# Routing of four expert layers: the gather by halves of the model columns, row products behind the first expert product, other filler counts, three and four down pieces outside the ring

## The chip, the cores and the metric

One core of one Trainium2 chip runs the whole program. The metric is the device time in microseconds of one execution; lower is better. Times of a few executions are given with their median. The profile is of one further execution, and all times inside it are counted from the start of its span.

The engines have the profile's names: PE is TensorE (matrix products), PEld its weight loads, DVE is VectorE, ACT is ScalarE, POOL is GpSimd, SP is SyncE, which here only issues transfers (DMA).

## The reference

Two blocks of two layers each work on 256 tokens of width 1024, in float32. Each layer is a mixer (a gated MLP, attention in several forms) followed by a mixture of experts. The four expert layers are called 0 to 3 here. Layers 0 and 1 (first block) have 32 experts, layers 2 and 3 (second block) have 16. What an expert layer computes, cut to what matters:

```python
def hierarchical_moe(h, ...):                  # h: rms-normed x, 256 x 1024
    g_prob = softmax(t @ w_group + b_group)     # 4 groups
    g_idx = argmax(g_prob); g_w = g_prob[g_idx]
    e_sel = (t @ w_expert + b_expert)[group g_idx]
    top_w, top_i = top_k(softmax(e_sel), 2)     # two experts of the group
    weights = g_w * top_w / sum(top_w)
    # combine: 256 x n_experts, two entries in a row
    gate, up = t @ w_gate[e], t @ w_up[e]       # 1024 -> 256 each
    y = sum_e (silu(gate) * up * combine[:, e]) @ w_down[e]   # 256 -> 1024
x = x + y                                       # second block: x + g_f * y
```

In the second block the normed rows are also scaled and shifted by vectors made from `c` (`w_ada`), and the layer's output is multiplied by a row `g_f`.

## The kernel before, in words

**Weights come as a stream.** All large weights are cut into chunks that SP loads, in one fixed order, into a ring of 24,576 floats in each partition (`Stream`, `ring`). A chunk waits until the chunks that lay in its place have been used: engines count the semaphore `chunk_used` up when they are done with some, and SP waits for a count ahead of each issue. In an expert layer a piece is 1 MiB, so that twelve pieces fill the ring. An expert has three: two with its gate and up weights (rows 0 to 511 and 512 to 1023 of the model columns) and one with its down weights. For the first two experts the down pieces lie outside the ring, in the tile `first_down` (`FIRST_DOWN = 2`, "aside").

**Routing, once in a layer (function `moe`).** PE transposes x (L1502), multiplies it by the router weights (L1514, and ends with `r_ready`), and then issues products of zeros into an unused bank (`keep_busy`, L359). DVE meanwhile picks group and experts (`picks_ready`). PE makes counts from the picks (L1526, L1527), issues twelve more fillers, and DVE makes from the counts the slot of each token for its experts: a one-hot matrix `gather` for each half `t` of the tokens. Then PE gathers the tokens into slots, `xn_split` times `gather` (L1538): for each half t of the tokens the eight blocks k of 128 model columns, two products each (the normed rows are kept as a high and a low part), into four banks. ACT takes banks 0 and 2 of a half (L1720), DVE banks 1 and 3 (`take_gathered`, L1869 or L1872), into `xsT`. PE then turns ranks and weights of the slots into rows (`rows_by_half`, L1546), which ACT copies (L1724, L1726). POOL copies the slots of the first two experts, a pair, out of `xsT` at places known only at run time (L1489): one window of 32 slots for each expert and half of the tokens, all eight k at once. Then the expert products begin.

**Experts, in pairs i.** `gate_up(i, 0)` and `gate_up(i, 1)` are the products over the first and the second four k (L1595); `turn` and `down(i)` (L1604, L1618) follow, and `combine` (L1633) adds rows back to tokens. Each engine branches once in a layer on whether no expert has over 32 slots; the path with windows is the one that the trace shows, the other computes every expert for every token.

**Order.** All instructions of an engine run in the order in which the program has them, held only by semaphores. On ACT the count up of `chunk_used` for the pieces of `gate_up(0, 0)` stands behind everything that ACT has before it. SP's order is: stream up to the layer, first_down, rest of the stream.

## Time and profile before

| | |
|---|---|
| median of 3 runs | 1597.15 us (1593.39 to 1597.97) |
| the profiled execution | 1590.39 us |
| its span | 1588.6 us |
| busy: PE, DVE, ACT, POOL | 1455.9, 758.0, 494.1, 100.9 us |
| moved by DMA | 467.19 MB, mean 294 GB/s |
| mean granted PE clock | 0.977 of full |

The span runs from the first to the last instruction; 1.8 us of the execution lie around it. The page's slices show the transfers at 420 GB/s in most of the expert layers and far below in the mixers, while PE is busy nearly throughout. "Busy" PE time has its waits for data between products left out only where they are long enough to show. The profiled execution is 6.8 us below the median of the runs.

### The profile page before, as it was taken

Reading aid. Unit: us, or ns where it says so; the run is one execution under the profiler, and the core shown is the slowest. Engines: PE = TensorE matmul, PEld = TensorE weight load, DVE = VectorE, ACT = ScalarE, POOL = GpSimd, SP = SyncE. Lnnn points to the kernel's source line nnn. Section 1 sums busy time; section 2 is a strip of 40 time slices with the busy share of each in tenths; the row PEclk is TensorE's granted clock in tenths of the full one; section 3 lists DMA queues with packets and bytes.
Section 4 is the critical chain, followed back from the end, with each engine's and each line's share of the span. In section 5 each row is a group of like instructions: output and inputs, shape, how many; then the busy total and the mean of one; then the engine's idle time right before and its main releaser. Section 6 shows DMA issues by size and latency. Waiting matters only on the chain. (4 is left out here: it accounts for less than half of the span.)

```text
span 1588.6 us, 23901 instructions
## 1 busy us (share of the span) xinstructions
PE 1455.9 (92%) x9314; PEld 808.2 (51%) x9314; DVE 758.0 (48%) x1618; ACT 494.1 (31%) x982; POOL 100.9 (6%) x242
## 2 busy tenths in 40 slices
PE   8999999888899898998888998999999979999997
PEld 4586533222375554322227876787663337756432
DVE  1656432222444635222236655775574346677433
ACT  3222211111215402111126655665412126551211
POOL 0000011010000001111101000100001101000110
PEclk9999999999999999999999998999989999998999
DMA  9985589999963186999997461435079996417996
GB/s 369 369 355 214 236 331 420 421 419 421 404 264 120 50 334 283 420 420 421 421 424 314 178 235 41 158 133 192 24 322 378 420 425 246 151 50 296 387 420 276
DMA packets 62391, 467.19 MB, mean 294 GB/s; under 512 B 7696, under 2 KB 15808, under 8 KB 17472
## 3 DMA queue, kind: packets, MB, share of 16 engines
q1 hardware_dynamic: 62272, 465.59, 72.5%
q8 instruction: 76, 1.25, 0.3%
q14 instruction: 43, 0.35, 0.1%
HBM read 462.81 MB, written 2.76 MB: 293 GB/s over the span
## 5 line engine op out<-in xcount | busy, mean ns | idle before, releaser
L1595 PE MATMUL PS<-ring,catT 128*32 128x512 f32 x3072 | 349.0, 596 | 29.5 <-issue 22.6
L793 PE MATMUL PS<-w_split,h_split 128*128 128x512 f32 x1152 | 271.0, 394 | 6.0 <-DVE w_split L878 6.0
L793 PEld LDWEIGHTS PS<-w_split,h_split 128*128 128x128 f32 x1152 | 214.2, 189 | 56.5 <-DVE w_split L878 8.5
L1595 PEld LDWEIGHTS PS<-ring,catT 128*32 128x32 f32 x3072 | 99.8, 110 | 247.2 <-issue 247.0
L1618 PE MATMUL PS<-ring,hidden_cols 128*32 128x512 f32 x1408 | 159.7, 593 | 29.6 <-issue 24.4
L878 DVE TENSOR_TENSOR w_split<-ring,w_split 128x512 fp32r<-128x512 f32 x192 | 132.7, 706 | 67.4 <-ACT w_split L826 67.2
L826 ACT CAST w_split<-ring 128x512 fp32r<-128x512 f32 x192 | 118.0, 619 | 105.1 <-PE PS L793 104.5
L1765 ACT ACTIVATE hidden_rows<-PS 128x256 f32<-128x256 f32 x48 | 18.5, 384 | 387.6 <-PE PS L1595 387.6
L1618 PEld LDWEIGHTS PS<-ring,hidden_cols 128*32 128x32 f32 x1408 | 47.8, 110 | 134.9 <-issue 134.8
L484 PE MATMUL PS<-ring,catT 128*128 128x512 f32 x224 | 100.8, 610 | 1.0 <-PEq L989 1.0
L413 DVE SCALAR_TENSOR_TENSOR ada_part<-ring,silu_c,ada_part 128x768 f32<-128x768 f32 x98 | 99.9, 1019 | 3.5
L1973 DVE SCALAR_TENSOR_TENSOR xn_split<-PS,slot_w,xn_split 128x512 fp32r<-128x512 f32 x64 | 48.1, 751 | 107.1 <-ACT xn_split L1753 107.0
L1489 POOL COPY catT<-xsT 128x256 f32 x192 | 69.5, 405 | 449.7 <-PE PS L1595 414.4
L1941 DVE TENSOR_TENSOR hidden_rows<-PS,hidden_rows 128x256 f32<-128x256 f32 x48 | 20.3, 422 | 134.4 <-ACT hidden_rows L1765 134.4
L1945 DVE COPY hidden_cols<-PS 128x256 f32<-128x256 f32 x48 | 20.4, 425 | 122.3 <-PE PS L1604 122.3
L1753 ACT ACTIVATE xn_split<-PS,slot_w 128x512 fp32r<-128x512 f32 x64 | 44.0, 688 | 103.3 <-PE PS L1618 103.3
L484 PEld LDWEIGHTS PS<-ring,catT 128*128 128x128 f32 x224 | 43.3, 195 | 54.1 <-issue 54.1
L1966 DVE SCALAR_TENSOR_TENSOR gated_rows<-PS,slot_w,grow 128x512 f32<-128x512 f32 x32 | 24.0, 751 | 83.0 <-PE PS L1618 83.0
L1702 ACT ACTIVATE xn_split<-x 128x1024 fp32r<-128x1024 f32 x8 | 8.5, 1059 | 165.3 <-PEq L454 115.0
L1633 PE MATMUL PS<-xn_split,back 64*128 64x512 f32 x384 | 57.4, 417 | 2.3 <-DVE xn_split L1976 2.1
L1458 POOL MEMSET xsT<- 128x512 f32 x4 | 2.1, 527 | 660.5 <-POOLq L454 524.6
L1633 PEld LDWEIGHTS PS<-xn_split,back 64*128 64x128 f32 x384 | 32.3, 184 | 18.3 <-issue 10.1
(420 smaller groups left out, 1754.1 us busy)
## 6 DMA issues: line engine op xcount, KB each, us to landing
ring<-in_moe SPq DMA_DIRECT2D x280, 1024.0 KB, 16.5
ring<-in_w_ada SPq DMA_DIRECT2D x16, 3072.0 KB, 11.5
ring<-in_a_w_in SPq DMA_DIRECT2D x23, 2048.0 KB, 12.4
ring<-in_b_w_in SPq DMA_DIRECT2D x8, 2048.0 KB, 22.1
first_down<-in_moe SPq DMA_DIRECT2D x8, 1024.0 KB, 17.6
ring<-in_a_w_out SPq DMA_DIRECT2D x2, 3072.0 KB, 10.8
ring<-in_b_w_out SPq DMA_DIRECT2D x2, 3072.0 KB, 9.9
ring<-in_w_mem_kv SPq DMA_DIRECT2D x2, 2048.0 KB, 11.4
```

Of the source, the lines that this page charges most:

```text
L413: dlink(nc.vector.scalar_tensor_tensor(part, w[:, k, :], silu_c[:, k:k + 1], part, ALU.mult, ALU.add))
L484: last = nc.tensor.matmul(PS[:, i % 8, 0:n], srcT[:, j, t * P:(t + 1) * P], w[:, j, o:o + n], start=j == 0, stop=j == k - 1)
L793: last = nc.tensor.matmul(PS[:, 2 * (i % 2) + t, :], hs[:, hp, k, t * P:(t + 1) * P], wk[:, (KT * i + k) % splits, wp, :], start=k == 0 an ...
L826: nc.scalar.copy(wk[:, (KT * i + k) % splits, 0, :], w[:, k, :]).then_inc(w_high.sem, 1)
L878: nc.vector.tensor_tensor(wk[:, (KT * i + k) % splits, 1, :], w[:, k, :], wk[:, (KT * i + k) % splits, 0, :].bitcast(F32), ALU.subtract).t ...
L1489: nc.gpsimd.tensor_copy(xf[:, i % 2, :, q * HALF:(q + 1) * HALF], padded(q // 2)[:, :, bass.ds(at, HALF)]).then_inc(win_ready.sem, 1)
L1595: last = nc.tensor.matmul(PS[lanes, 4 + i % 2, :].rearrange("p (g f) -> p g f", g=2), xf[:, i % 2, k, lanes], gate_up_weights(2 * i + q % ...
L1618: last = nc.tensor.matmul(PS[lanes, 6 + c, :], hs[:, i % 2, f2, lanes], down_weights(2 * i + q % 2)[:, f2, c * BANK:(c + 1) * BANK], start ...
L1633: last = nc.tensor.matmul(PS[:, 2 * t + c, :], back[lanes, i % 2, :], yk(i, h, c)[lanes], start=i == 0 and h == 0, stop=i == NP - 1 and h ...
L1753: nc.scalar.activation(yk(i, 0, c), PS[:, 6 + c, :], ACT.Copy, scale=slot_w[:, i % 2, :]).then_inc(y_high.sem, 1)
L1966: nc.vector.scalar_tensor_tensor(gated[:, c, :], PS[:, 6 + c, :], slot_w[:, i % 2, :], grow[:, c * BANK:(c + 1) * BANK], ALU.mult, ALU.mul ...
L1973: nc.vector.scalar_tensor_tensor(yk(i, 1, c), PS[:, 6 + c, :], slot_w[:, i % 2, :], high, ALU.mult, ALU.subtract).then_inc(y_low.sem, 1)
```

## The change

All in `moe` and what it calls:

- **Gather by halves of the columns.** PE makes for k 0 to 3 both halves of the tokens first, then for k 4 to 7. ACT and DVE take the banks in that order. POOL copies the first pair's windows in two sets of four, with four k each (`first_windows`), and `gate_up(0, 0)` waits for the first set only, `gate_up(0, 1)` for the second. The banks of the second half of the tokens are 4, 5, 6, 7 where they were 6, 7, 4, 5.
- **Row products and weight chain later.** `rows_by_half` for ranks and weights (now `ranks_and_weights`) stands between `gate_up(0, 0)` and `gate_up(0, 1)`; DVE makes ranks and weights after it has taken all banks; ACT copies the rows behind its table load, ahead of the first count up of `chunk_used`.
- **Fillers.** In layers 2 and 3 three instead of ten stand between L1519 and the counts.
- **Down pieces aside.** Three in layer 0, four in layer 1, two in layers 2 and 3. The third (expert 2) goes into `hT`, once the router has read it (`r_ready`); the fourth into `mem_kv`, the tile of the memory's keys and values, which are no longer read after the mixer of layer 1. The path for crowded experts makes its `hT` anew, in `h_again`.

```diff
-FIRST_DOWN = 2
+ASIDE = (3, 4, 2, 2)
-            XB = ((0, 1, 2, 3), (6, 7, 4, 5))
+            XB = ((0, 1, 2, 3), (4, 5, 6, 7))
...
-                aside = FIRST_DOWN
-                first_down = sbuf(st, "first_down", [P, aside, PIECE])
+                aside = ASIDE[m]
+                first_down = sbuf(st, "first_down", [P, 2, PIECE])
+                aside_at = [first_down[:, 0, :], first_down[:, 1, :], hT[:].rearrange("p k t -> p (k t)"), mem_kv[:]][0:aside]
...
-                    for e in range(aside):
-                        nc.sync.dma_start(first_down[:, e, :], A[f"moe{m}"][e][:, 2 * PIECE:3 * PIECE]).then_inc(down_loaded.sem, 16)
+                    for e in sorted(range(aside), key=lambda e: e == 2):
+                        if e == 2:
+                            sp.wait_ge(*r_ready.at(1))
+                        nc.sync.dma_start(aside_at[e], A[f"moe{m}"][e][:, 2 * PIECE:3 * PIECE]).then_inc(down_loaded.sem, 16)
                     stream.issue(nc, sp, first + 3 * E - aside)
...
+                    def first_windows(starts):
+                        pool.wait_ge(*tail_zeroed.at(1))
+                        for h in range(2):
+                            ks = slice(4 * h, 4 * h + 4)
+                            for q, at in enumerate(starts):
+                                if q % 2 == 0:
+                                    pool.wait_ge(*xs_taken_act.at(2 * h + q // 2 + 1))
+                                    pool.wait_ge(*xs_taken_dve.at(2 * h + q // 2 + 1))
+                                nc.gpsimd.tensor_copy(xf[:, 0, ks, q * HALF:(q + 1) * HALF], padded(q // 2)[:, ks, bass.ds(at, HALF)]).then_inc(win_ready.sem, 1)
...
-                    keep_busy(3, 18 if gate is None else 10)
+                    keep_busy(3, 18 if gate is None else 3)
...
-                    for t in range(TT):
-                        pe.wait_ge(*xn_low.at(t + 1))
-                        pe.wait_ge(*gather_ready.at(t + 1))
-                        for b in range(KT // 2):
...
+                    for h in range(2):
+                        for t in range(TT):
+                            if h == 0:
+                                pe.wait_ge(*xn_low.at(t + 1))
+                                pe.wait_ge(*gather_ready.at(t + 1))
+                            elif t == 1 and gate is not None:
+                                pe.wait_ge(*gate_taken.at(1))
+                            for b in (2 * h, 2 * h + 1):
...
+                        if i == 0 and half_of_k == 1:
+                            pe.wait_ge(*win_ready.at(8))
                         if half_of_k == 0:
-                            pe.wait_ge(*win_ready.at(4 * (i + 1)))
+                            pe.wait_ge(*win_ready.at(4 * (i + 1) + (4 if i else 0)))
...
                     gate_up(0, 0)
+                    ranks_and_weights()
                     gate_up(0, 1)
...
-                            if c == 1 and 2 * i >= aside:
-                                nc.scalar.sem_inc(chunk_used, 2)
+                            if c == 1 and 2 * i + 1 >= aside:
+                                nc.scalar.sem_inc(chunk_used, 2 if 2 * i >= aside else 1)
...
                     nc.scalar.activation(stat[:, 2, 30:31], ones_f[:, 0:1], ACT.Silu)
+                    take_ranks_and_weights(act)
                     for i in range(NP):
                         act.wait_ge(*half_ready.at(i + 1))
                         nc.scalar.sem_inc(chunk_used, 2)
...
-                    nc.vector.tensor_scalar(sc[:, 10:12, :], sc[:, 8:10, :], 1.0, None, ALU.add).then_inc(rank_made.sem, 1)
...
-                    take_gathered(0)
+                    for h in range(2):
+                        for t in range(TT):
+                            take_gathered(h, t)
+                    nc.vector.tensor_scalar(sc[:, 10:12, :], sc[:, 8:10, :], 1.0, None, ALU.add).then_inc(rank_made.sem, 1)
...
-                    take_gathered(1)
```

PE's program in layer 2, from the first fillers to the row products, before (`zero` is the fillers' operand, `picks` the picked experts, `gather` the one-hot matrix, `rsc` the ranks and weights):

```order
L359 MATMUL PS<-zero 128x512 x10
L1526 MATMUL PS<-picks,before 128x32 [waits picks_ready]
L1527 MATMUL PS<-picks,ones_b 128x32
L359 MATMUL PS<-zero 128x512 x12
L1538 MATMUL PS<-gather,xn_split 128x256 [waits gather_ready,xn_low,gate_taken]
L1538 MATMUL PS<-gather,xn_split 128x256 x15
L1538 MATMUL PS<-gather,xn_split 128x256 [waits gather_ready,xn_low]
L1538 MATMUL PS<-gather,xn_split 128x256 x15
L1546 MATMUL PS<-ident,rsc 64x128 [waits xs_taken,rank_made]
L1546 MATMUL PS<-ident,rsc 64x128 x3
L1546 MATMUL PS<-ident,rsc 64x128 [waits xs_taken_dve,weight_made]
L1546 MATMUL PS<-ident,rsc 64x128 x3
```

The same stretch after, to the last gather product:

```order
L360 MATMUL PS<-zero 128x512 x3
L1536 MATMUL PS<-picks,before 128x32 [waits picks_ready]
L1537 MATMUL PS<-picks,ones_b 128x32
L360 MATMUL PS<-zero 128x512 x12
L1550 MATMUL PS<-gather,xn_split 128x256 [waits gather_ready,xn_low]
L1550 MATMUL PS<-gather,xn_split 128x256 x7
L1550 MATMUL PS<-gather,xn_split 128x256 [waits gather_ready,xn_low]
L1550 MATMUL PS<-gather,xn_split 128x256 x15
L1550 MATMUL PS<-gather,xn_split 128x256 [waits gate_taken]
L1550 MATMUL PS<-gather,xn_split 128x256 x7
```

Seven fillers (now L360) are gone, the wait for `gate_taken` has moved from the first gather product (now L1550) to the last eight, and the row products no longer follow here. Where they are now, in layer 0, from the branch on (L1611 is the gate and up product, L1558 the row products):

```order
L1434 TENSOR_LOAD table [waits table_ready]
L1434 ISA x2
L1697 COMPARE_AND_BRANCH
L1611 MATMUL PS<-ring,catT 32x512 [waits window_ready,chunk_loaded0,chunk_loaded15]
L1611 MATMUL PS<-ring,catT 32x512 x15
L1558 MATMUL PS<-ident,rsc 64x128 [waits xs_taken,rank_made]
L1558 MATMUL PS<-ident,rsc 64x128 x3
L1558 MATMUL PS<-ident,rsc 64x128 [waits xs_taken_dve,weight_made]
L1558 MATMUL PS<-ident,rsc 64x128 x3
L1611 MATMUL PS<-ring,catT 32x512 [waits window_ready,chunk_loaded2,chunk_loaded1]
```

The first half of the first pair's product stands right behind the branch, the row products behind it, and the second half waits for a second set of windows. ACT in layer 0 before, from the last bank taken to the first SiLU (`hidden_rows`; the counts up of `chunk_used` are not printed, the first stands between the two waits of the last row):

```order
L1720 ACTIVATE xsT<-PS,cols 128x256
L1724 COPY catT<-PS 128x256 [waits rank_rows]
L1726 COPY catT<-PS 128x256 [waits slot_weight_ready]
L1431 TENSOR_LOAD table [waits table_ready]
L1431 ISA x2
L1741 COMPARE_AND_BRANCH
L1759 ACT_TABLE_LOAD
L1759 ACTIVATE stat<-ones_f 128x1
L1765 ACTIVATE hidden_rows<-PS 128x256 [waits gate_up_half_ready,gate_up_ready] x2
```

and after:

```order
L1747 ACTIVATE xsT<-PS,cols 128x256
L1434 TENSOR_LOAD table [waits table_ready]
L1434 ISA x2
L1773 COMPARE_AND_BRANCH
L1791 ACT_TABLE_LOAD
L1791 ACTIVATE stat<-ones_f 128x1
L1754 COPY catT<-PS 128x256 [waits rank_rows]
L1756 COPY catT<-PS 128x256 [waits slot_weight_ready]
L1798 ACTIVATE hidden_rows<-PS 128x256 [waits gate_up_half_ready,gate_up_ready] x2
```

The two copies of the rows have moved behind the branch and the table load, and stand directly ahead of the wait for the half product and of the count up behind it.

## Rows read from the trace of the kernel before

**Rows 1.** Page, 40 equal slices of the span: GB/s moved.
```profile
GB/s 369 369 355 214 236 331 420 421 419 421 404 264 120 50 334 283 420 420 421 421 424 314 178 235 41 158 133 192 24 322 378 420 425 246 151 50 296 387 420 276
```

**Rows 2.** Windows, layer 0; busy PE, PEld, DVE, ACT, POOL; clock, DMA share, GB/s.
```profile
210.00:410.00 200.00, 178.49 (x1546) 58.43 (x1542) 48.17 (x118) 25.03 (x43) 19.20 (x54) 0.99 1.01 421
```

**Rows 3.** Timeline, TensorE, second to last down product of layer 2.
```profile
1289.91 3.64 PE L1618 MATMUL PS<-ring,hidden_cols 128*32 128x512 f32 x32 [1.28 <-issue]
```

**Rows 4.** Timeline, TensorE, second to last down product of layer 3.
```profile
1569.12 3.64 PE L1618 MATMUL PS<-ring,hidden_cols 128*32 128x512 f32 x32 [0.99 <-issue]
```

**Rows 5.** Timeline, SyncE, experts of layer 0: all issues from the first on.
```profile
205.60 184.19 SPq L95 DMA_DIRECT2D ring<-in_moe  x82
```

**Rows 6.** Windows, the transfers at rest, layers 0 to 3; columns of rows 2.
```profile
192.20:206.50 14.30, 12.50 (x106) 7.60 (x110) 10.38 (x37) 5.80 (x13) 3.19 (x9) 1.00 0.01 3
606.00:618.40 12.40, 10.60 (x97) 6.71 (x99) 9.15 (x31) 5.60 (x12) 3.11 (x8) 1.00 0.02 6
1203.60:1206.50 2.90, 2.90 (x32) 1.06 (x28) 0.39 (x1) 0.00 (x0) 1.34 (x4) 1.00 0.06 20
1484.00:1486.80 2.80, 2.80 (x31) 0.94 (x24) 0.24 (x1) 0.00 (x0) 1.19 (x4) 1.00 0.08 26
```

**Rows 7.** Timeline, all engines, routing of layer 0.
```profile
181.73 3.92 PE L1514 MATMUL PS<-wr,hT 128*128 128x36 f32 x32
...
192.16 0.20 PE L1526 MATMUL PS<-picks,before 128*128 128x64 bf16 x1 [2.62 <-DVE picks L1840]
...
192.43 0.23 DVE L1844 COPY tot<-PS 128x64 f32<-128x64 f32 x1 [0.26 <-PE PS L1527]
...
195.58 4.06 PE L1538 MATMUL PS<-gather,xn_split 128*128 128x256 f32 x32 [0.60 <-DVE gather L1856]
...
196.33 3.71 ACT L1720 ACTIVATE xsT<-PS,cols 128x256 f32<-128x256 f32 x8 [3.92 <-PE PS L1538]
...
196.97 1.49 DVE L1869 TENSOR_TENSOR xsT<-PS,cols 128x512 f32<-128x512 f32 x2
...
199.57 1.09 PE L1546 MATMUL PS<-ident,rsc 128*64 128x128 f32 x16
...
200.71 0.37 ACT L1726 COPY catT<-PS 128x256 f32<-128x256 f32 x1
200.96 0.76 POOL L1489 COPY catT<-xsT 128x256 f32 x2 [1.49 <-DVE xsT L1869]
201.62 1.28 ACT L1759 ACT_TABLE_LOAD   x1 [0.54 <-issue]
...
201.86 8.36 PE L1595 MATMUL PS<-ring,catT 128*32 128x512 f32 x76 [1.20 <-POOL catT L1489]
```

**Rows 8.** Timeline, all engines, routing of layer 2.
```profile
1188.39 3.27 PE L359 MATMUL PS<-zero 128*128 128x512 bf16 x10
...
1191.74 0.19 DVE L1844 COPY tot<-PS 128x32 f32<-128x32 f32 x1 [1.84 <-PE PS L1527]
...
1194.60 4.07 PE L1538 MATMUL PS<-gather,xn_split 128*128 128x256 f32 x32 [0.29 <-DVE gather L1856]
...
1201.84 8.74 PE L1595 MATMUL PS<-ring,catT 128*32 128x512 f32 x77 [2.16 <-POOL catT L1489]
```

**Rows 9.** Timeline, all engines, routing of layer 3.
```profile
1472.08 0.19 DVE L1844 COPY tot<-PS 128x32 f32<-128x32 f32 x1 [1.41 <-PE PS L1527]
...
1474.94 4.06 PE L1538 MATMUL PS<-gather,xn_split 128*128 128x256 f32 x32 [0.29 <-DVE gather L1856]
...
1482.10 4.49 PE L1595 MATMUL PS<-ring,catT 128*32 128x512 f32 x39 [2.08 <-POOL catT L1489]
```

**Rows 10.** Windows, around the fillers of layer 2; columns of rows 2.
```profile
1186.00:1188.00 2.00, 2.00 (x12) 2.00 (x11) 1.69 (x11) 0.00 (x0) 0.00 (x0) 0.50 1.00 422
1190.00:1191.00 1.00, 1.00 (x5) 0.45 (x4) 0.00 (x0) 0.99 (x2) 0.00 (x0) 0.85 0.95 401
```

**Rows 11.** Timeline, TensorE, experts of layer 0: start us, us, what, [idle before].
```profile
339.74 5.34 PE L1595 MATMUL PS<-ring,catT 128*32 128x512 f32 x32 [2.46 <-issue]
```

More of the change, by code:

```diff
@@ L1415, in down_weights @@
                 def down_weights(e):
-                    w = first_down[:, e, :] if e < aside else stream.raw(piece(e, 2))
+                    w = aside_at[e] if e < aside else stream.raw(piece(e, 2))
                     return w.rearrange("p (k f) -> p k f", k=2)
@@ L1477, in _ @@
                     nc.switch_bb(f"slots_{m}")
-                    for i in range(NP):
-                        if i:
-                            starts = windows(i)
+                    first_windows(starts)
+                    for i in range(1, NP):
+                        starts = windows(i)
                         if i >= 2:
```

112 lines of the change are left out of this document (63 added, 49 removed).

## The prediction

> **What bounds the kernel now.** PE is busy 1455.9 of the span's 1588.6 us by the page's first part, but its slices, which I read next, divide the program: the transfers run at 420 GB/s in four stretches, those of the expert layers, and fall far below between them [rows 1]. The mixers are bound by PE and what feeds it, the expert stages by the stream of weights. A window over layer 0 has a DMA share of 1.01 while PE lacks 21.5 of 200 us [rows 2]; layer 1 has as many pieces at the same rate. In layers 2 and 3, half as long, the 14 pieces fetched ahead nearly last, and PE lacks little but 1.28 and 0.99 us at the second to last down product [rows 3, 4]. There both limits are close, and the stream ends last.
>
> Since the stream is the limit, I looked next for the times at which it stands still with work left. In layer 0 SP issues nothing more for the ring until 205.60, when ACT has given back the first two places [rows 5]; 82 pieces are left. The transfers end at 192.2 and flow again at 206.5 [rows 6]. The same hole is 12.4 us in layer 1, but only 2.9 and 2.8 us in layers 2 and 3. It is the key to the sum: in layers 0 and 1 each piece more that lands in the hole, and each microsecond by which the first place comes free earlier, moves the end of the stage; in layers 2 and 3 nothing can move it by more than the hole.
>
> Then the timeline of the routing, for what ends the hole. In layer 0 the gather products start at 195.58 and take 4.06 us, PE makes the row products to 200.66, ACT, DVE and POOL take and copy, and the first expert product starts at 201.86, let go by POOL [rows 7]. Its first half is 32 products of 110 ns (8.36 us for 76), 3.5 us, and ends at 205.35; SP issues 0.25 us later, and the flow starts 1.2 us after PE's end.
>
> **The change, part by part.** Call S the start of the first expert product.
>
> *Gather by halves.* The same 32 products, in another order, so their sum stays 4.06 us. After half of them, 2.03 us, everything for the first half product is in PSUM. In layer 0 that is 197.6. ACT needs for its two banks half of 3.71 us from 196.33, so 198.2; DVE has its two banks' worth in 1.49 us from about 196.9, so 198.4; POOL then copies two windows of half the size, at most the 0.76 us of two full ones [rows 7], at least half of that: 199.0 to 199.4. PE is done with the gather at 199.64. So S follows the gather itself and POOL is no longer waited for. What is newly uncovered is the load of the table's entry and the branch on PE, which hid under the wait for POOL. They are at most the 1.2 us between the last row product and S; ACT, with the same instructions, idles 0.54 us ahead of its table load, and the low end is 0, if PE's sequencer does them while products run. I take 0.3. S = 199.94, 1.9 us earlier (1.0 to 2.2). Layer 1 is the same to 0.1 us.
>
> A figure of the Trainium skill speaks against this term: DMA: Bandwidth & Descriptors, in the section on latency and other measured facts, gives a floor of about 600 ns for such a load. By it S would gain 1.6 in place of 1.9 us; no row shows PE's load alone, and ACT's 0.54 us lies just under it.
>
> *Row products behind the first half.* 1.09 us of PE [rows 7] leave the shadow of the wait and stand on PE's path, between two halves. Their inputs are ready: DVE takes four banks at 0.75 us to about 200.4, and adds ranks and weights; before, its first takes ended at 198.46 and PE's row products, which wait for the weights, began at 199.57, so these chains take under 1.4 us together: 201.8, and PE asks at 203.4. The second set of windows is ready by then as well. The point that costs is on ACT. ACT's two copies of these rows now stand ahead of its first count up of `chunk_used`, so the ring's first places come free not at the end of the first half product but behind the row products, 1.09 us later, and behind up to one copy of 0.37 us; I take 0.2. The first release gains 1.9 − 1.1 − 0.2 = 0.6 us in layers 0 and 1 (−0.5 to 1.1).
>
> The next release, at the second half product's end, follows 3.5 us later, and two pieces take 5.0 us (1.05 MB at 421 GB/s is 2.49 us a piece), so the flow holds. In layer 1, where two down products give nothing back, PE frees the 13th place eight products after the first, 28 us and the small steps between them, and the stream wants it after 12 pieces, 30 us: just enough, with a stall of some tenths possible.
>
> *Pieces aside.* Each is one piece less for the stream after the hole, 2.5 us. The one in `hT` can be issued when the router's products end, at 185.65 in layer 0, while the transfers are still busy until 192.2 [rows 6, 7]; it lands by 195, in the hole. In layer 1 two pieces end at 611, and the hole lasts to 618. So 2.5 and 5.0 us, each with nothing behind: SP waits only where it would wait for the ring. With a later flow elsewhere it could be 0 (rival 2). Below it there is no cost; the down product that uses them comes 15 us after S.
>
> *Fillers.* In layer 2 DVE's first step after the counts waits 1.84 us for PE, in layer 3 1.41 us, in layer 0 0.26 [rows 7 to 9]: PE is busy with fillers when the picks come. Ten take 3.27 us in layer 2, the first ones at half clock, an estimated 0.43 each; three end at 1189.7, before the picks, which are there at 1189.9. Gain 1.6 and 1.15 us. The gather then starts at 1193.0 and 1473.8, and S = start + 4.06 + 0.3 = 1197.4 and 1478.15, against 1201.84 and 1482.10: 4.4 and 3.95 us. POOL is not in the way: two sets shorter than the 0.76 us above.
>
> What the stream gets of it is S's gain less 1.3: 3.1, cut to the hole of 2.9, and 2.65. PE's own chain gains S less 1.1: 3.3 and 2.85, more than that, so the stream stays last. Layers 2 and 3: 2.9 + 2.65 = 5.55 us. The last pair's steps follow the down product that waited [rows 3, 4] and move with it.
>
> *Other bank numbers, the keys and values in one tile, the dense path's own `hT`*: not executed differently, 0. The mixers after each stage start from the stage's end, and the stream there is shifted by the same time, so nothing is given back.
>
> **Sum.** Layer 0: 0.6 + 2.5 = 3.1. Layer 1: 0.6 + 5.0 = 5.6. Layers 2 and 3: 5.55. Together 14.25 us of 1590.4, 0.9%: 1576.1 for an execution like the profiled one. The profiled one is 6.8 us under the median of the runs; taken from the median, 1597.15 − 14.25 = 1582.9. With the low ends (release −0.5 twice; a branch of 1.2 us in layers 2 and 3 takes 0.7 and 0.9 more) it is 10.4 us, with the high ends (release 1.1, holes full) 15.4.
>
> **Rivals.**
>
> 1. *The half clock lasts over the gather in layers 2 and 3.* The granted clock in layer 2 is 0.50, 1.2 GHz, over the small products ahead of the fillers, and goes to 2.4 GHz in the third microsecond of fillers (0.85 in that window) [rows 10]. With three fillers, a short pause and twelve more the rise could come later. At half clock the twelve fillers behind the counts take 5.1 us, 2.3 more than the 2.86 that DVE takes from the counts to the gather [rows 8], so S gains 2.1 and 1.65, the stream 0.8 and 0.35: the total is 8.7 + 1.15 = 9.85 us, 1587.3. If the gather is slow too, 4.06 us more, the stream loses 3.3 and 3.7 there: total 1.7, 1595.4. Against it: in layer 0 PE is idle 2.6 us ahead of the counts [rows 7] and the gather still runs in 4.06 us, at 2.4 GHz, and the pause here is some tenths. The Trainium skill's rule (TensorE: Matmul & The Clock Gate, part 1), that the throttled state is the default and activity releases it, is the reason why I keep this case; the trace agrees in that the clock rose under the fillers, and not in layer 0, where idleness did not lower it.
>
> 2. *The places come free too late for the extra pieces.* The ring stalls in layer 1, or the pieces aside only change which one PE waits for. For it: the 13th place is tight. Against: the transfers run at 1.01 for 200 us with PE lacking 11% of its time, so a piece less must end earlier. If half of the 7.5 us are lost: 10.5 us, 1586.7; if all, 1590.4.
>
> 3. *Slower.* The half clock of layers 2 and 3 holds until the first pair's two half products are done. A half product took 5.34 us once, behind a wait of 2.46 us [rows 11], against 3.5, 1.8 us more. To the 6.4 us of rival 1 come 1.8 for the first half product and 1.1 for row products at twice their time: the first release is 4.4 − 1.3 − 9.3 = −6.2 us early in layer 2 and −6.65 in layer 3, and every further one, 5.3 us behind the one before, is 0.3 us too slow for the stream. Together some 13.5 us lost against 8.7 gained: 1601.9. It decides from the point where each of the layers 2 and 3 loses over 4.35 us at its first release, that is, when the clock rises only inside the first half product.
>
> 4. *The row products stay hidden and the release is free of the copies*, or PE's fillers gave more: 17 us, 1580.
>
> **How the numbers follow.** Forecast 0.63; rival 1 0.14, of it 0.04 with the slow gather; rival 2 0.10; rival 3 0.03; rival 4 0.10. The likeliest case's own range is 1580 to 1587. The median has its own spread of about 2 us either way. The range 1577 to 1591 holds the forecast, rival 4, the mild part of rival 1 and rival 2; left out are the slow gather, rival 3 and outer errors. A difference of 0.3%, 4.8 us, is about what a measurement of this kernel can tell: faster by more than that are the forecast and rival 4 (0.73), the mild part of rival 1 (0.10) and 0.08 of rival 2: 0.91. Within it: the slow gather and the rest of rival 2, 0.06. Slower: rival 3, with a hold that lasts a little longer than worked out, 0.03.
>
> **What would show it.** In the changed profile: the hole of layer 0 from about 194.7 to 205.9, of layer 1 from 611 to 618 in today's times, and none or under 0.3 us in layers 2 and 3. The first expert product 0.3 us behind the last gather product, with no wait for POOL. Row products 3.5 us later, without a wait. SP's first issue behind ACT's weight copy, about 4.9 us after S. In layers 2 and 3 a wait of DVE for the counts of 0.3 us, and granted clock 1.00 over the gather. Waits of PE in the experts of layers 0 and 1 that sum to 2.3 and 4.8 us less. Wrong it would be if the stages of layers 0 and 1 end as late after their routing as before, if the clock in layers 2 and 3 is 0.50 when the gather starts, or if a wait on `chunk_used` opens a new hole in layer 1 some 30 us after the first release.

## The result and the profile after

The changed kernel takes 1580.3 us in the median of eight runs (1569.5 to 1587.7), the kernel before 1596.5 us in eight runs of the same session (1593.3 to 1598.9). The ratio is 0.9907 with a 95% interval of 0.9882 to 0.9932. Run again later as it is, it took 1578.2 us against 1595.5 us, ratio 0.9890 (0.9868 to 0.9913). The profiled execution took 1578.0 us with a span of 1576.3 us, at a mean granted clock of 0.975; before it was 1590.4, 1588.6 and 0.977.

The page's slices first, GB/s moved, as in [rows 1]. The four flat stretches at 420 are there again. The fifth and the sixteenth slice, in which the holes of layers 0 and 1 begin or lie, are fuller, 275 for 236 and 342 for 283, and in the fourteenth, inside a mixer, 5 are left of 50: the stream is ahead and has less to bring there.

```profile
GB/s 359 392 351 205 275 315 420 421 421 421 427 301 111 5 324 342 412 420 421 420 424 306 171 240 43 129 165 177 40 243 415 420 423 262 205 40 278 417 420 275
```

Then the hole in each layer. [rows 6] measured it between its own ends; to compare kernels I now use windows at a fixed distance from the layer's first transpose, 12 to 30 us behind it in layers 0 and 1, 24 to 30 us in layers 2 and 3. First the kernel before, in the order of the layers (busy time of PE, PEld, DVE, ACT, POOL, then clock, DMA share, GB/s):

```profile
191.96:209.96 18.00, 16.00 (x138) 8.90 (x142) 11.02 (x40) 6.18 (x14) 4.03 (x12) 1.00 0.20 70
603.91:621.91 18.00, 15.99 (x138) 8.91 (x142) 11.23 (x40) 6.18 (x14) 4.16 (x12) 1.00 0.31 112
1201.13:1207.13 6.00, 5.29 (x52) 2.05 (x56) 2.62 (x10) 0.78 (x2) 2.11 (x6) 1.00 0.52 187
1481.49:1487.49 6.00, 5.39 (x52) 2.07 (x56) 2.52 (x10) 0.74 (x2) 2.03 (x6) 1.00 0.55 193
```

and the changed kernel:

```profile
193.06:211.06 18.00, 17.20 (x150) 8.68 (x154) 11.43 (x40) 6.18 (x14) 5.26 (x17) 1.00 0.41 157
601.28:619.28 18.00, 17.40 (x151) 8.76 (x153) 11.10 (x40) 6.18 (x14) 5.20 (x17) 1.00 0.62 247
1199.52:1205.52 6.00, 6.00 (x68) 2.35 (x68) 2.08 (x7) 1.13 (x3) 2.39 (x7) 1.00 0.96 369
1471.93:1477.93 6.00, 6.00 (x66) 2.17 (x66) 1.54 (x6) 1.13 (x3) 2.58 (x8) 1.00 0.95 386
```

GB/s times the window's length gives what was moved: 1.57 MB more in layer 0 (87 GB/s over 18 us), 2.43 MB in layer 1, 1.09 and 1.16 MB in layers 2 and 3. At the 421 GB/s of [rows 2] that is 3.7, 5.8, 2.6 and 2.8 us, together 14.9 us by which the stream is ahead once the hole is over.

How the hole ends in layer 0: TensorE, then ScalarE, GpSimd and SyncE in the timeline, which answer to [rows 7].

```profile
196.68 4.07 PE L1550 MATMUL PS<-gather,xn_split 128*128 128x256 f32 x32 [0.60 <-DVE gather L1889]
200.67 3.64 PE L1611 MATMUL PS<-ring,catT 128*32 128x512 f32 x32
204.25 1.09 PE L1558 MATMUL PS<-ident,rsc 128*64 128x128 f32 x16
...
204.95 0.37 ACT L1754 COPY catT<-PS 128x256 f32<-128x256 f32 x1 [2.23 <-PE PS L1558]
205.38 0.37 ACT L1756 COPY catT<-PS 128x256 f32<-128x256 f32 x1
...
199.79 0.54 POOL L1468 COPY catT<-xsT 128x128 f32 x2 [0.28 <-DVE xsT L1901]
...
205.43 181.68 SPq L95 DMA_DIRECT2D ring<-in_moe  x81
```

The first expert product (L1611) starts 3.99 us behind the gather's start with no idle time ahead of it; before it was 6.28 us, of it 1.20 us of waiting for POOL. The row products (L1558) follow 3.6 us later, also without a wait. SP issues 4.76 us behind the first expert product, 8.75 us behind the gather's start; before it was 10.02.

In layers 2 and 3, TensorE and the one step of VectorE that waits for the counts (layer 2, then layer 3), for [rows 8] and [rows 9]:

```profile
1187.88 0.64 PE L360 MATMUL PS<-zero 128*128 128x512 bf16 x2 [0.22 <-issue]
1188.94 0.19 PE L1536 MATMUL PS<-picks,before 128*128 128x32 bf16 x1 [0.42 <-DVE picks L1873]
...
1189.19 0.19 DVE L1877 COPY tot<-PS 128x32 f32<-128x32 f32 x1 [0.24 <-PE PS L1537]
...
1192.04 4.07 PE L1550 MATMUL PS<-gather,xn_split 128*128 128x256 f32 x32 [0.28 <-DVE gather L1889]
...
1460.75 0.21 PE L1536 MATMUL PS<-picks,before 128*128 128x32 bf16 x1
...
1461.02 0.19 DVE L1877 COPY tot<-PS 128x32 f32<-128x32 f32 x1 [0.26 <-PE PS L1537]
...
1463.87 4.07 PE L1550 MATMUL PS<-gather,xn_split 128*128 128x256 f32 x32 [0.21 <-DVE gather L1889]
```

DVE's waits of 1.84 and 1.41 us are 0.24 and 0.26 us, and the gather runs at its full speed of 4.07 us.

**The layers' own times.** For every kernel I took from the timeline of its one profile the time from a layer's first transpose of x to the start of its last step of combine products. Two executions of one kernel (changed and e5, e3 and e8, e7 and e9) differ in a layer by up to 0.8 us, once by 1.9. "Time x clock" is the mean, over a kernel's runs, of each run's time multiplied by its mean granted clock; what it is for is told below.

| kernel | layer 0 | 1 | 2 | 3 | sum | median of runs | ratio to before (95%) | time x clock |
|---|---|---|---|---|---|---|---|---|
| before | 238.3 | 238.2 | 124.7 | 123.6 | 724.8 | 1594.6 / 1595.5 / 1593.9 | | 1551.0 / 1550.5 / 1552.5 |
| changed | 234.6 | 234.3 | 121.6 | 121.6 | 712.1 | 1580.3 | 0.9907 (0.9882 to 0.9932) | 1538.2 |
| changed, again (e5) | 234.4 | 234.5 | 120.9 | 120.8 | 710.6 | 1578.2 | 0.9890 (0.9868 to 0.9913) | 1536.8 |
| two aside (e1) | 237.8 | 237.6 | 121.1 | 120.9 | 717.4 | 1589.0 | 0.9962 (0.9944 to 0.9980) | 1544.5 |
| ten fillers (e2) | 234.7 | 234.8 | 121.6 | 121.7 | 712.8 | 1578.8 | 0.9907 (0.9880 to 0.9934) | 1539.7 |
| release first (e3) | 234.8 | 232.9 | 120.1 | 120.9 | 708.7 | 1574.4 | 0.9876 (0.9854 to 0.9898) | 1534.3 |
| by tokens (e4) | 236.2 | 234.8 | 121.0 | 122.5 | 714.5 | 1581.8 | 0.9929 (0.9905 to 0.9953) | 1540.3 |
| three aside in layer 1 (e6) | 235.4 | 234.8 | 122.4 | 120.4 | 713.0 | 1582.5 | 0.9924 (0.9903 to 0.9944) | 1540.7 |
| rows back (e7) | 234.7 | 232.5 | 121.0 | 123.1 | 711.3 | 1581.6 | 0.9917 (0.9900 to 0.9934) | 1535.9 |
| release first, again (e8) | 234.6 | 232.8 | 120.1 | 120.1 | 707.6 | 1575.0 | 0.9872 (0.9851 to 0.9893) | 1534.6 |
| rows back, again (e9) | 234.6 | 233.1 | 120.8 | 121.3 | 709.8 | 1577.6 | 0.9899 (0.9851 to 0.9946) | 1537.1 |
| release first, three aside (e10) | 234.5 | 234.4 | 122.6 | 120.1 | 711.6 | 1579.5 | 0.9916 (0.9881 to 0.9950) | 1537.0 |

The times before stand for the three sessions: e1 to e4, e5 to e8, e9 and e10. The change's 12.7 us in the sum are all of the 12.3 us between the two spans: the start is 1.1 us later, the three mixers between the layers together 0.1 us longer, the rest behind layer 3 0.8 us shorter.

The mixers' 0.1 us hides something, though. The mixer ahead of layer 2 is 5.0 us longer, the one ahead of layer 3 4.9 us shorter, and the change touches neither. The granted clock tells them apart. Two windows in the mixer ahead of layer 2, of the kernel before:

```profile
983.00:1003.00 20.00, 15.59 (x114) 12.66 (x111) 11.80 (x18) 10.06 (x22) 8.67 (x8) 1.00 0.08 14
...
1103.00:1123.00 20.00, 16.49 (x134) 12.12 (x136) 12.97 (x35) 12.80 (x31) 0.00 (x0) 0.91 0.37 119
```

and of the changed one:

```profile
983.00:1003.00 20.00, 17.33 (x90) 14.28 (x87) 11.52 (x17) 10.56 (x20) 8.36 (x8) 0.91 0.26 92
...
1103.00:1123.00 20.00, 19.05 (x147) 14.65 (x148) 9.05 (x24) 10.40 (x26) 0.00 (x0) 0.75 0.24 76
```

The mixer ahead of layer 3 is the reverse case, 0.95 before and 0.98 after over its whole length. A share of 0.75 over 20 us means 10 us at 1.2 GHz, 0.91 means 3.6 us. Work that is bound by PE and has 10 us at half clock loses 5 us. These stretches come at other places from execution to execution, and they carry a large part of the scatter: the eight runs go from 1569.5 us at a mean clock of 0.979 to 1587.7 us at 0.969. Time x clock is, as far as work at half clock takes twice as long, what an execution would take with the clock always full, and in the six runs of e5 it spans 3.2 us (1535.3 to 1538.5) where the times span 11.2. It doesn't remove all scatter, though. In the first eight runs it still spans 8.2 us where the times span 18.2, and in e7, e8 and e10 it spans more than the times do (6.9, 5.5 and 10.0 us against 5.4, 4.7 and 7.0). Over all 95 runs, each kernel around its own mean in its session, the clock accounts for about 60% of the variance of the times. Against the fourteen runs of the changed kernel (mean 1537.6) a difference in the last column is uncertain by 1.3 to 3.5 us (95%, an estimate from the scatter of the runs), most where a kernel has four runs.

### The profile page after: what moved, and what is told of

Its sections match the earlier page's. It is cut to its first block and busy times, and to the rows that moved or that the text cites. A ratio compares the mean times of both kernels' runs of the same rounds, so it can differ in the third digit from the quotient of the medians.

```text
span 1576.3 us, 23913 instructions
## 1 busy us (share of the span) xinstructions
PE 1455.5 (92%) x9293; PEld 808.9 (51%) x9300; DVE 757.3 (48%) x1618; ACT 494.1 (31%) x982; POOL 102.9 (7%) x258
## 5 line engine op out<-in xcount | busy, mean ns | idle before, releaser
L1611 PE MATMUL PS<-ring,catT 128*32 128x512 f32 x3072 | 348.1, 594 | 22.3 <-issue 21.0
L1611 PEld LDWEIGHTS PS<-ring,catT 128*32 128x32 f32 x3072 | 96.5, 110 | 239.0 <-issue 238.8
L1634 PE MATMUL PS<-ring,hidden_cols 128*32 128x512 f32 x1360 | 156.0, 593 | 27.5 <-issue 22.2
L1499 POOL COPY catT<-xsT 128x256 f32 x176 | 63.3, 403 | 411.6 <-PE PS L1611 404.0
L1649 PEld LDWEIGHTS PS<-xn_split,back 64*128 64x128 f32 x384 | 32.3, 184 | 18.2 <-issue 10.1
## 6 DMA issues: line engine op xcount, KB each, us to landing
ring<-in_w_ada SPq DMA_DIRECT2D x16, 3072.0 KB, 13.7
```

The source lines that it names most:

```text
L1499: nc.gpsimd.tensor_copy(xf[:, i % 2, :, q * HALF:(q + 1) * HALF], padded(q // 2)[:, :, bass.ds(at, HALF)]).then_inc(win_ready.sem, 1)
L1611: last = nc.tensor.matmul(PS[lanes, 4 + i % 2, :].rearrange("p (g f) -> p g f", g=2), xf[:, i % 2, k, lanes], gate_up_weights(2 * i + q % ...
L1634: last = nc.tensor.matmul(PS[lanes, 6 + c, :], hs[:, i % 2, f2, lanes], down_weights(2 * i + q % 2)[:, f2, c * BANK:(c + 1) * BANK], start ...
L1649: last = nc.tensor.matmul(PS[:, 2 * t + c, :], back[lanes, i % 2, :], yk(i, h, c)[lanes], start=i == 0 and h == 0, stop=i == NP - 1 and h ...
```

## The experiments

**e1, the pieces aside undone.** What each of the two parts, asides and routing, is worth alone.

```
-ASIDE = (3, 4, 2, 2)
+ASIDE = (2, 2, 2, 2)
```

> The change with two down pieces aside in every layer. Stage time is counted from the first transpose of x to the start of the last combine product; with the change it was 234.6, 234.3, 118.9, 118.9 us in layers 0 to 3. Theory (each piece aside is 2.5 us of a stream that sets the end): layer 0 237.1; layer 1 237.8 to 239.3, as the fourth piece brought a stall of the ring of about 1.2 us with it, which goes too; layers 2 and 3 the same within 0.5 us. The whole 5 to 7.5 us slower than the change. Rival (the pieces only change what PE waits for): stages 0 and 1 within 0.5 us of the change's. In the waits the difference must be PE idling ahead of half and down products.

Measured: 1589.0 us, 6.3 to 7.7 us above the changed kernel's two sets of runs by time x clock. Layer 1, where the first product comes at the same distance as with the change, is the clean place: in its window

```profile
604.25:622.25 18.00, 17.40 (x151) 8.75 (x153) 11.09 (x40) 6.18 (x14) 5.18 (x17) 1.00 0.34 129
```

129 GB/s in place of 247 are 2.12 MB, two pieces of 1.05 MB, missing from the hole. The layer is 3.3 us longer, not 5.0, and just below the theory's 3.5. Layer 0 lost 3.2 us, for 2.5 in the theory, but 0.6 of it lies ahead of the gather's end, where this execution had half clock. So the third piece of layer 0 is worth about 2.5 us, the third and fourth of layer 1 together 3.3, and the routing alone is the 0.5 and 0.6 us that layers 0 and 1 still gain (1.1 in layer 0 without its half clock), plus all of layers 2 and 3. The rival, that the pieces only change what PE waits for, is refuted.

**e2, ten fillers again in layers 2 and 3.**

```
-                    keep_busy(3, 18 if gate is None else 3)
+                    keep_busy(3, 18 if gate is None else 10)
```

> The change with ten fillers in layers 2 and 3 again, not three. Theory: the counts start 1.5 us later, S (the start of the first expert product) is 1.5 us later against the stage's start, and the ring's first release with it; since the release with the change comes about 1.3 us (layer 2) and nothing (layer 3) ahead of the end of the transfers fetched ahead, the stages get longer by 0.7 to 1.5 us each, 2 to 3 us in all. Rival (three fillers leave the clock low in some executions, and cause the wide spread of the changed kernel's times, 1569 to 1588): no median change or a gain, the spread shrinks to that of before (5 us), and granted clocks over the gather differ. If the spread stays, it has another place.

Measured: the first expert product starts 21.5 us behind the layer's start in both layers in place of 20.6 and 20.0, and the layers take 121.6 and 121.7 us, against 121.6 and 121.6 (120.9 and 120.8 in e5). The hole opens a little:

```profile
1200.27:1206.27 6.00, 6.00 (x64) 2.21 (x60) 2.43 (x10) 0.83 (x3) 1.47 (x5) 1.00 0.84 313
1472.67:1478.67 6.00, 6.00 (x64) 2.21 (x60) 2.45 (x10) 0.81 (x3) 1.45 (x5) 1.00 0.87 321
```

That is 0.34 and 0.39 MB less than with three, 0.8 and 0.9 us. The fewer fillers are worth 0 to 0.9 us a layer by the layers' times, 1.5 to 2.9 us together by time x clock, and nothing by the medians, so that their worth is hardly clear of noise. It is the smaller part of a change that moved S by 4.1 and 4.6 us there. The halves and the row products alone nearly close the hole. On the rival: the gather runs at full clock with ten fillers and with three, so three don't leave the clock low there; the four runs lie 6.2 us apart, too few to say whether the spread shrank.

**e3 and e8, the ring's first places given back ahead of the row copies.** ACT counts up first and copies then.

```
-                    take_ranks_and_weights(act)
                     for i in range(NP):
                         act.wait_ge(*half_ready.at(i + 1))
                         nc.scalar.sem_inc(chunk_used, 2)
+                        if i == 0:
+                            take_ranks_and_weights(act)
```

> The change with ACT's count up for the first half product ahead of its copies of the row products, nothing else moved. Theory (the stream starts again when ACT counts up): SP's first issue 1.2 us earlier against S, 3.6 us behind it, not 4.8; stage 0 shorter by 1.2 us (233.4); stage 1 about the same, since the 13th place comes no earlier and the stall there grows by what the start gains; stages 2 and 3 within 0.4 us, their hole being closed. Rival (PE's own chain sets the stage): stage 0 the same.

> ScalarE frees the first two ring slots ahead of its two row copies, as in an earlier run, now in more rounds and beside the changed kernel. Theory (slots freed 1.0 us earlier shorten the hole of layers 0 and 1 by 1.0 to 1.3 us each and close the 0.3 us left in layers 2 and 3): time times mean clock 2 to 4 us below the changed kernel's of the same session, the median 1572 to 1578 us. Rival (the lower time of the earlier run was a run of higher clocks only): time times clock within 1 us of the changed kernel's.

Measured twice: SP issues 3.75 us behind S in place of 4.76, and the time is 1574.4 and 1575.0 us, 3.1 us (e8 against e5) below the changed kernel by the medians and 2.2 by time x clock. Both sets of four together lie 3.2 us below the fourteen runs of the changed kernel by time x clock, uncertain by 2.0. This is the fastest version of the study, although the intervals of its ratio and the changed kernel's overlap. The windows of e8, layers 1 and 2:

```profile
602.33:620.33 18.00, 17.18 (x150) 8.68 (x154) 11.09 (x40) 6.17 (x14) 5.22 (x17) 1.00 0.71 285
...
1197.58:1203.58 6.00, 6.00 (x68) 2.38 (x68) 2.05 (x7) 1.13 (x3) 2.40 (x7) 1.00 1.04 427
```

The hole of layer 2 is gone and the layer 0.8 to 1.5 us shorter; layer 1 gains 1.3 to 1.7 us. Layer 0 gained nothing (234.8 and 234.6), though its hole is 1.1 us shorter (183 GB/s over the 18 us in place of 157). That is the number of e3's rival in layer 0, and e3's theory had the two layers the wrong way round, 1.2 us in layer 0 and nothing in layer 1; e8's had 1.0 to 1.3 us in both. So an earlier release moved the end of layer 1 here and not that of layer 0, and no run shows why.

**e4, the gather by token halves, windows still in two parts.** The loops over `h` and `t` are exchanged on PE, ACT and DVE, and the counts that ACT, DVE and POOL wait for follow; the rest stays.

```
-                    for h in range(2):
-                        for t in range(TT):
+                    for t in range(TT):
+                        for h in range(2):
```

> The change with the gather products, and ACT's and DVE's takes, in the order of before (all eight k of one half of the tokens, then of the other), but POOL's windows still in two sets of four k. Tells what the order of the gather gives, and what the split windows alone. Theory: the first set needs six of eight banks, 3.05 us after the gather's start, then DVE 0.7 and POOL 0.7: S at 4.4 to 4.7 us after the gather's start, where the change has 4.0 and before had 6.3. So the order is worth only 0.4 to 0.7 us, and stages 0 and 1 get longer by that; stages 2 and 3, where DVE takes 0.95 a bank, S at 5.0 or so, stage longer by 0 to 0.7. Rival (the order is the cause): S at 5.5 to 6.3 and stages 0 and 1 longer by over 1.5 us.

Measured: PE waits for POOL again, in layer 0 and layer 2:

```profile
201.51 1.92 PE L1611 MATMUL PS<-ring,catT 128*32 128x512 f32 x16 [0.68 <-POOL catT L1468]
...
1194.77 2.78 PE L1611 MATMUL PS<-ring,catT 128*32 128x512 f32 x24 [0.99 <-POOL catT L1468]
```

The first product starts 4.8 to 5.3 us behind the gather's start in place of 4.0 to 4.1. Layer 0 loses 1.6 us (0.6 of it to half clock over the gather, 4.65 us in place of 4.07), layer 1 0.3 to 0.5, layer 3 0.9 to 1.7, and time x clock is 2.1 to 3.5 us up, no more than its uncertainty. The theory fits layer 1 (first product at 4.7 us) and S in layers 2 and 3 (5.0 us), but layers 0 and 3 lose more than its 0.7 us; the rival wanted the first product at 5.5 us or later and over 1.5 us in both layers 0 and 1, and that didn't come. By these numbers the order by model columns is worth 2 to 3.5 us of the 13, not clear of noise in the whole; what it does to the first product is.

**e5, the changed kernel again.**

> The changed kernel itself, once more, beside the next three. Its eight runs so far lie 18 us apart (1569.5 to 1587.7) and follow the mean granted clock (0.979 to 0.969). If the clock is the whole of that scatter, the product of time and mean clock of each run stays within about 2 us of its mean so far (1538), whatever the time is, and the median lies within 1574 to 1586. If something else moves (transfers, the order of landings), the product scatters as widely as the time.

Measured: 1578.2 us, time x clock 1536.8. The six products lie within 2.7 us of 1538, as the first theory has it in the main. That holds for these runs, not for all sets, as told above: the clock is the larger part of the scatter, and the rest is open.

**e6 and e10, three pieces aside in layer 1**, without and with the early release of e3.

```
-ASIDE = (3, 4, 2, 2)
+ASIDE = (3, 3, 2, 2)
```

> Layer 1 keeps three down pieces aside in place of four, all else as in the changed kernel. Theory (a piece aside fills 2.5 us of the hole in which nothing is transferred, less what comes late afterwards): the hole of layer 1 grows from 6.9 to 9.4 us, the short dips of the transfers 62 us into the layer (0.3 us, where the ring waits for a slot) go away, and the layer's time grows from 234.3 to 236.0 to 236.8 us; the whole is 1.7 to 2.5 us longer. Rival (the fourth piece was past the point where the ring pays, so that it only moved the wait): layer 1 stays within 0.5 us of 234.3 us.

> ScalarE frees the first ring slots ahead of its row copies, and layer 1 keeps three pieces aside, not four. With four pieces and the early release layer 1 took 232.9 and 232.8 us. Theory (the fourth piece is worth its 2.5 us in the hole, but the last down piece lands later relative to the bytes moved once the ring has run full, which takes some of it back): the hole is 7.5 to 8 us, no dips around 55 to 62 us, the bytes from the layer's start to its last down product 92.6 to 92.7 MB in place of 93.0, layer 1 takes 233.8 to 234.6 us. Rival A (the fourth piece is worth all of 2.5 us): 235.3 us. Rival B (it is worth nothing): 232.9 us.

Measured, the window of layer 1, e6:

```profile
604.82:622.82 18.00, 17.18 (x150) 8.66 (x154) 11.10 (x40) 6.18 (x14) 5.23 (x17) 1.00 0.51 197
```

197 GB/s are 1.10 MB less than e5's 258: one piece, 2.6 us. But layer 1 is only 0.3 to 0.5 us longer in e6, which is the rival's number, and 1.5 to 1.7 us longer in e10 than in e3 and e8, which lies within the theory's. The fourth piece is worth 0.3 to 1.7 us there. The two numbers come nearer to each other when the slips of the stream (told with e7 and e9) are taken out: they sum to 0.7 us in e6's layer 1 and 1.4 in e5's, but to 1.5 and 1.6 in those of e10 and e8, which leaves about 1.0 and 1.7 us. Something that nobody forecast comes on top: layer 2 takes 122.4 and 122.6 us in the two kernels with three aside, against 120.1 to 121.6 in all other versions of the changed kernel. In both, layer 2 moves 48.3 to 48.4 MB to the start of its last down product, in e5 and e8 47.4 MB, and 24 to 30 us into it e6 moves 418 GB/s where e5 has 371. So about one piece less seems to have been fetched ahead when the layer began, an estimated 2.1 to 2.4 us. One piece more in the ring moves the place of every later chunk, which may be the reason; it isn't shown, and e1, with three pieces more in the ring, does not have it (121.1 us). By time x clock the fourth piece is worth 3.9 us in all (e6 against e5) and 2.4 us (e10 against e8), more than layer 1 shows; the second is uncertain by more than itself, and in the first 1.0 us lies in layer 0, which no edit touched: e6's gather there ran partly at half clock, 4.60 us in place of 4.06. The dips behind the hole in layer 1 did go away (0.32 us of them in the changed kernel, 62 us into the layer). The bytes moved from the layer's start to its last down product, 93.0 MB, did not fall as e10's theory had it: they are 92.9 MB.

**e7 and e9, the row products back ahead of the first expert product**, on PE, DVE and ACT. DVE makes the ranks ahead of its takes and the weights behind the first one; the lines that are put in elsewhere are left out here.

```
                     gate_up(0, 0)
-                    ranks_and_weights()
                     gate_up(0, 1)
...
-                    for h in range(2):
-                        for t in range(TT):
-                            take_gathered(h, t)
-                    nc.vector.tensor_scalar(sc[:, 10:12, :], sc[:, 8:10, :], 1.0, None, ALU.add).then_inc(rank_made.sem, 1)
+                    take_gathered(0, 0)
```

> The row products of ranks and weights go back ahead of the first expert product, on TensorE, VectorE and ScalarE, all else as in the changed kernel. The first expert product then starts 5.1 to 5.9 us behind the gather's start in place of 4.0, but ScalarE has its two copies behind it and frees the first ring slots 3.75 us behind that product in place of 4.76. Theory (what counts in layers 0 and 1 is when the first slots are freed, and in layers 2 and 3 the hole is closed either way): slots are freed 8.8 to 9.6 us behind the gather's start in place of 8.75, and the layers' times grow by 0 to 0.8 us each in layers 0 and 1 and by under 0.3 us in layers 2 and 3, together 0 to 2 us. Rival (the start of the first product is what counts): 1.1 to 1.9 us in each of the four layers, 4.4 to 7.6 us together.

> The row products ahead of the first expert product, once more. In the earlier run layer 1 took 232.5 us with them there, against 234.3 and 234.5 us in two profiles of the changed kernel, though the first ring slots came free at the same distance from the layer's start (24.4 us) and the hole was the same (6.5 us). Theory (the place of the row products has a price of its own in layer 1: it brings on the dips of the transfers 62 us into the layer, 0.3 us, and the last down piece then lands 0.4 to 0.7 MB late): 232.3 to 232.9 us again, with under 0.1 us of dips there. Rival (scatter of single executions): 233.8 to 235 us this time.

Measured, e7, layer 0:

```profile
196.13 4.06 PE L1550 MATMUL PS<-gather,xn_split 128*128 128x256 f32 x32 [0.60 <-DVE gather L1888]
200.11 1.09 PE L1558 MATMUL PS<-ident,rsc 128*64 128x128 f32 x16
201.25 2.34 PE L1613 MATMUL PS<-ring,catT 128*32 128x512 f32 x18
...
204.98 0.80 SPq L95 DMA_DIRECT2D ring<-in_moe  x2
```

The first expert product starts 1.1 us later and SP issues 8.85 us behind the gather's start, as good as 8.75. The kernel is not slower for it: time x clock 1535.9 and 1537.1 against 1536.8. By the medians it is 3.4 us above (e7 against e5) and 0.6 below (e9 against e5), by time x clock both together are 1.2 us below the changed kernel's fourteen runs, uncertain by 2.1. The rival, that the first product's start counts, wanted 1.1 us or more in every layer and 4.4 together, and is refuted. One layer missed the theory too: layer 3 took 123.1 us in e7, 1.6 to 2.3 more than in the changed kernel, where under 0.3 was expected. 10.2 us of half clock in its routing, 6.8 in the others, put its gather 17.4 us into the layer, in e9 16.6; there the layer took 121.3 us. This part of the change brings nothing as it stands; with the release ahead of the copies (e3, e8) it does.

Layer 1 was 232.5 and 233.1 us, not 234.3 to 234.8; the second time lies between e9's two theories. The steps in which PE waits for pieces show where. From about 120 us into the layer on (109 before the change), every second step waits, and each pair of pieces comes 4.97 us behind the one before (1.05 MB twice at 422 GB/s). Once a layer that pace slips: by 1.1 us at 200 us and 0.4 at 226 in the changed kernel's layer 1, by 1.4 us in layer 1 of before, by 1.3 to 1.7 us in layer 0 of every kernel. In layer 1 of e7 and e9 the slips come to 0.4 and 0.3 us. Why they have the smaller one stays open; the dips near 62 us into the layer, which e9's theory made the cause, are there in e9 too (0.2 us).

## Why the prediction was right

The forecast was 1583.0 us, range 1577 to 1591; the median is 1580.3. Of 14.25 us, 12.3 came in the two profiles and 12.8 to 13.7 by time x clock. The medians differ by more, 16.2 and 17.4 us; in the session of e5 the runs of the changed kernel had a mean clock of 0.9738 and those of before 0.9720, which is 2.9 us of it. That the median lies only 2.7 us from the forecast is therefore in part luck: it is nearer still to rival 4's 1580, whose mechanism, a release free of the copies, is not there. And in the layers two errors of opposite sign meet: layer 0 gained 3.7 us for 3.1, layer 1 3.9 for 5.6, layers 2 and 3 5.1 for 5.55, together 12.7 for 14.25.

*The hole is the key: right in the main.* The stream got 14.9 us ahead in the four windows, against 14.25 forecast, and e7 shows that the release, not the first product, sets it. What failed is that each microsecond by which the first place comes free earlier moves the end of the stage in layers 0 and 1: in layer 0 of e3 and e8 1.0 us did not.

*Release in layers 0 and 1: mis-sized.* Forecast 0.6 us, 1.1 at most; it came 1.27 us earlier relative to the gather. S gained 2.29 us for 1.9, and the copies took 0.3 less than forecast. The load and the branch on PE, put at 0.3 us with 1.2 as the high end, cost nothing that the timeline shows: the first product starts before the last gather product's modelled end. The trace of the changed kernel lists the load by itself (shortest, median and longest of the four in ns, start of the first and the last):

```profile
L1434 PEldq TENSOR_LOAD <-table x4: 300/310/484, 198.4 to 1465.6; - x4
```

In layer 0 it runs from 198.45 to 198.93, inside the gather, whose last product ends at 200.75. The floor of about 600 ns that the Trainium skill gives for such a load (DMA: Bandwidth & Descriptors, latency and other measured facts) is above what was measured here, 0.30 to 0.48 us, and the load is not on PE's path.

ACT's two copies delay the release by 1.01 us, about what the row products alone would (1.09), in place of 1.3. SP issues 0.05 us behind the start of the second copy. In layer 1 about half of the 1.27 us was lost again in this execution, since most of the first fillers ran at half clock,

```profile
595.94 6.27 PE L360 MATMUL PS<-zero 128*128 128x512 bf16 x17 [0.22 <-issue]
```

against 3.83 us for the same 17 in layer 0, and the counts came 0.56 us later. In e5 the first fillers were done 0.97 us ahead of the picks and the counts came in time.

*Pieces aside: right in the hole, too large at the layer's end.* Each brought its 1.05 MB there. Layer 0 shortened with it, by 3.7 us where 3.1 were forecast. In layer 1 the term 5.0 us failed: 5.6 us were forecast, 5.8 us were gained in the hole, and 3.9 and 3.7 us arrived at the end. Rival 2 named this, with half of the gain lost; about a third was, in one layer. The step of the prediction that failed here is "each with nothing behind", that a piece brought forward in the hole shortens the layer by its whole 2.5 us; e1 gives the two pieces 3.3 us, not 5.0. From the layer's first transpose to the start of its last down product the two kernels move, before and then changed,

```profile
591.91:826.58 234.67, 206.24 (x1777) 74.99 (x1778) 70.35 (x190) 38.74 (x68) 23.91 (x66) 1.00 0.96 395
```
```profile
589.28:819.98 230.70, 208.86 (x1776) 75.53 (x1778) 70.22 (x190) 38.74 (x68) 24.44 (x70) 0.99 0.98 403
```

That is 92.7 and 93.0 MB: about 0.3 to 0.4 MB more, 0.7 to 1.0 us, had gone through when the last pieces were there. In e5 it is 93.3 MB: its hole window has 258 GB/s, 6.2 us ahead of the kernel before, and the layer gained 3.7 all the same. Another 0.3 us are the dips at the 13th place, which the prediction held possible. The rest of the shortfall against the forecast, some 0.5 us, is within the scatter of the layer's slips. That earlier bytes do not all turn into earlier last pieces is shown (layer 0 of e3 and e8 too); why is open.

*Layers 2 and 3: right.* 2.9 + 2.65 us forecast; 3.1 and 2.0 us in the first profile, 3.8 and 2.8 in the second. S gained 4.1 and 4.6 us (forecast 4.4 and 3.95), in the second profile 4.1 and 3.9. The clock was full over the gather, so rivals 1 and 3 are out. A rest of the hole of about 0.3 us stayed in each and went only with the early release.

*Points of "what would show it".* The hole of layer 0 lasted from about 195.7 to 206.4, as forecast but for the start of the span, 1.1 us later. No wait for POOL; row products 3.6 us behind S; SP 4.76 us behind S, forecast 4.9. From the first expert product on, PE's waits fell by 0.9 and 3.0 us where 2.3 and 4.8 were forecast (2.1 and 4.2 only with the 1.20 us of waiting for POOL ahead of it counted in). In layer 1 that is the shortfall again. In layer 0 the layer still shortened as told: before, one half product there ran in 5.34 us behind a wait [rows 11] and PE lost 1.7 us to half clock, which the changed execution did not.

## What to carry to other kernels

Where a stream of weights is the limit, look for the time in which it stands still, and ask which release ends it: in e7 PE's first product moved by 1.1 us and time x clock did not, in e3 and e8 one count moved past two copies and 2 to 3 us came, though none of it in layer 0. Put the count up for freed buffers ahead of everything else on its engine. Bytes brought forward are an upper bound for the gain, layer by layer (5.8 us in the hole, 3.9 at the end), and a changed number of pieces in a ring may show in a later layer too (layer 2 of e6 and e10). When the scatter follows the granted clock, compare time x clock and the stages' own times: the medians put e7 3.4 us above the changed kernel, both of these put it level. Neither is free of scatter: four runs hardly settle a difference under 2 or 3 us.

## What was not expected of the hardware

- A register load and a branch on PE between two sets of products showed no gap: 3.99 us from the gather's start to the next product, with a gather of 4.07 us. The load took 0.48 us and ended 1.7 us ahead of that product.
- ScalarE's semaphore count behind a copy took effect while that copy of 0.37 us had run 0.05 us (205.38 and 205.43).
- The pace at which pieces of the saturated stream land is even to some hundredths of a microsecond, 4.97 us for two, but slips once or twice a layer by 0.3 to 1.7 us in all, in every kernel. The cause is open.
- Granted half clock comes at different places in the mixers from one execution to the next: 10 us of it cost 5 us, and the mean clock accounts for about 60% of the variance of all runs. It also comes in the routing: the gather of layer 0 took 4.6 to 4.7 us in e1, e4 and e6 in place of 4.07.
